# Attention in a two-layer block: the next head pair's projections cut into eight pieces and laid between the steps of the current pair

## The reference

```python
qkv = (a_lat @ w_qkv)                        # 512 x 3072: q, k, v of 16 heads of 64
kv_c = (a_ctx @ w_qkv[:, d:])                # 256 x 2048: k, v of the context
def attend_row(r):                           # 8 grid rows of 64 columns, in 4 column blocks n
    s_loc = einsum(q_row, k_slab) * scale + bias     # 8 x 32 keys around the block
    s_ctx = einsum(q_row, k_c) * scale               # 256 keys
    p = softmax(concatenate([s_loc, s_ctx], -1))
    o = einsum(p_loc, v_slab) + einsum(p_ctx, v_c)
y_lat = o @ w_o
x = x + g1 * rms_norm(y_lat, mix_post_g)     # then the feed-forward network
```

## Time and profile before

| | us |
|---|---|
| median of 3 runs | 1869.67 (1868.39 to 1873.04) |
| the profiled execution | 1864.36 |
| its span in the trace | 1862.6 |
| TensorE busy | 1703.6 (91%) |
| ACT / POOL / DVE busy | 751.0 / 796.4 / 580.4 |
| the eight pairs of the attention | 1099 to 1407 of the span |
| mean granted TensorE clock | 0.964 |

### The profile page before, as it was taken

The page is one execution under the profiler, slowest core; times in us unless marked ns, Lnnn a source line. Parts: engine busy times, 40 slices in busy tenths (PEclk is TensorE's granted clock), DMA queues, the critical chain, the costliest instruction groups (busy, mean ns, idle before and its releaser), DMA issues.

```text
span 1862.6 us, 26862 instructions
## 1 busy us (share of the span) xinstructions
PE 1703.6 (91%) x9877; PEld 1319.2 (71%) x9877; DVE 580.4 (31%) x1122; ACT 751.0 (40%) x1142; POOL 796.4 (43%) x436
## 2 busy tenths in 40 slices
PE   5799999778989999999999799999989699999996
PEld 1566555266889998888888577777767488888884
DVE  2331130154566213334300233444340533333002
ACT  2322331153667544444422233444444444444220
POOL 0444332153567974444455523333225244444551
PEclk9899999888999999999999999999999799999998
DMA  8577787621445652323233211111212033233321
GB/s 315 189 231 245 263 260 249 227 91 57 124 140 176 188 175 90 91 91 100 86 94 93 70 34 41 40 40 45 81 39 77 26 106 97 90 95 91 94 82 46
DMA packets 70655, 222.08 MB, mean 119 GB/s; under 512 B 7856, under 2 KB 15408, under 8 KB 70320
## 3 DMA queue, kind: packets, MB, share of 16 engines
q1 hardware_dynamic: 69568, 217.29, 37.2%
q10 hardware_dynamic: 1008, 3.69, 0.5%
HBM read 215.44 MB, written 5.51 MB: 119 GB/s over the span
## 4 chain that ended last, share of the span: by engine, by line
PE 75%; issue 6%; DVE 6%; DMA 5%; ACT 3%; POOL 2%; SPq 1%; DVEq 1%; ACTq 0%; POOLq 0%
PE bank L1364 21%; PE bank L1365 21%; PE bank L1366 21%; PE bank L1334 3%; PE bank L1309 2%; DMA w_raw<-in_cv_w_pw 2%; POOL w_lo L539 2%; DVE probs L1262 1%; DMA ada_raw<-in_mod_w 1%; PE bank L1492 1%; PE bank L1379 1%; PE bank L1623 1%; PE bank L1634 1%; PE bank L1611 1%; PE bank L1470 1%
## 5 line engine op out<-in xcount | busy, mean ns | idle before, releaser
L539 POOL TENSOR_TENSOR w_lo<-w_raw,w_hi 128x1024 fp32r<-128x1024 f32 (+1 forms) x284 | 671.2, 2368 | 835.3 <-ACT w_hi L683 834.8
L1364 PE MATMUL bank<-h_hi_lat,w_hi 128*128 128x512 f32 x1056 | 423.1, 401 | 8.3 <-DVE h_lo_lat L1084 8.3
L1365 PE MATMUL bank<-h_lo_lat,w_hi 128*128 128x512 f32 x1056 | 419.4, 397 | 0.0
L1366 PE MATMUL bank<-h_hi_lat,w_lo 128*128 128x512 f32 x1056 | 418.9, 397 | 0.0
L683 ACT ACTIVATE w_hi<-w_raw 128x1024 fp32r<-128x1024 f32 (+1 forms) x284 | 295.3, 1040 | 275.5 <-DMA w_raw<-in_cv_w_pw 139.8
L1364 PEld LDWEIGHTS bank<-h_hi_lat,w_hi 128*128 128x128 f32 x1056 | 199.7, 189 | 67.6 <-issue 11.3
L1366 PEld LDWEIGHTS bank<-h_hi_lat,w_lo 128*128 128x128 f32 x1056 | 199.6, 189 | 48.3
L1365 PEld LDWEIGHTS bank<-h_lo_lat,w_hi 128*128 128x128 f32 x1056 | 199.8, 189 | 46.8
L1364 PE MATMUL bank<-h_hi_ctx,w_hi 128*128 128x256 f32 x672 | 194.9, 290 | 25.3 <-DVE h_lo_ctx L1056 10.2
L1365 PE MATMUL bank<-h_lo_ctx,w_hi 128*128 128x256 f32 x672 | 190.9, 284 | 0.0
L1366 PE MATMUL bank<-h_hi_ctx,w_lo 128*128 128x256 f32 x672 | 190.8, 284 | 0.0
(11 more groups left out here) (172 smaller groups left out, 2194.2 us busy)
## 6 DMA issues: line engine op xcount, KB each, us to landing
w_raw<-in_ffn_w_up SPq DMA_DIRECT2D x132, 512.0 KB, 3.6
ada_raw<-in_mod_w SPq DMA_DIRECT2D x96, 512.0 KB, 5.5
w_raw<-in_cv_w_pw SPq DMA_DIRECT2D x48, 512.0 KB, 6.9
w_raw<-in_ffn_w_down SPq DMA_DIRECT2D x48, 448.0 KB, 3.4
w_raw<-in_ffn_w_down SPq DMA_DIRECT2D x24, 512.0 KB, 3.6
w_raw<-in_na_w_qkv SPq DMA_DIRECT2D x24, 512.0 KB, 6.1
shifted_lat<-u_lat SPq DMA_DIRECT2D x32, 270.0 KB, 4.7
shifted_ctx<-u_ctx SPq DMA_DIRECT2D x32, 142.0 KB, 2.9
```

The lines of the kernel that those rows point to most:

```text
L539: pool.tensor_tensor(wlo[s][:, 0:kt * P], raw[s][:, 0:kt * P], whi[s][:, 0:kt * P].bitcast(F32), ALU.subtract).then_inc(w_lo, 1)
L1364: pe.matmul(b, whi[s][:, w], hi[:, a], start=(first and k == 0), stop=False)
L1365: pe.matmul(b, whi[s][:, w], lo[:, a], start=False, stop=False)
L1366: ins = pe.matmul(b, wlo[s][:, w], hi[:, a], start=False, stop=(last and k == kts - 1))
```

## The change

TensorE: the products of pair m + 1 are cut into eight pieces (`pair_products`): values in two halves of four k tiles, context values, keys in two halves, context keys, queries in two halves. Piece by piece they stand between the transposes, scores and weighted sums of pair m, three to each n; the places 8 to 10 take the three parts of turn_v. Values come first, queries last (the weight blocks are loaded in that order as well). Score(n + 1) follows turn_p(2n), and score(0) of the next pair stands before the last turn_p. In the last pair the nine free places take 7 of 8 k tiles of each of the first three blocks of "o" (`o_part`), where one block was begun before. ACT: the three copies out of PSUM, each with its rounding of weights, stand behind pt_copy 1, 3 and 5; the first two exponentials of the next pair stand behind pt_copy 6 and ahead of pt_copy 7, and behind pt_copy 7. DVE: take_max goes in twos, and the first two tiles of the next pair are done before `o_lo` of this one. POOL: the bias tables come before the last `w_lo` of the pair instead of after it. Banks: scores always in 5 and 6, transposed probabilities in 7 and 3, values and queries in 0, context in 1, keys and turned values in 2.

`qkv_products` falls away whole; of it, and of other long removed runs, nothing is shown here, since the functions before stand above.

```diff
-        SCORES = [[bank[5], bank[6]], [bank[0], bank[1]]]
-        TURNED = [bank[7], bank[2]]
-        V_TURNED = bank[3]
+        V_BANK, CTX_BANK, K_BANK, Q_BANK = bank[0], bank[1], bank[2], bank[0]
+        Q_FIRST = bank[3]
+        SCORES = [bank[5], bank[6]]
+        TURNED = [bank[7], bank[3]]
+        V_TURNED = bank[2]
...
                 for j in range(ph.per):
-                    lo_ahead(ph, it, j, last)
                     mj = j // 3
                     if j % 3 == 2 and not (isinstance(it, int) and it == 0 and mj == 0):
                         for hp in range(2):
                             pool.wait_ge(s_max, it * 16 + (8 * mj - 8 + 7 + hp + 2))
                             head_bias(it * 2 + mj, hp)
+                    lo_ahead(ph, it, j, last)
             loop(pool, ph, qkv_body, cuts=(1,))
...
-            def qkv_evac(m, q, b):
-                act.wait_ge(blk, b(1))
+            def v_out(q):
+                for n in range(NB):
+                    ins = act.activation(vT[q][:, n * WIN:(n + 1) * WIN].rearrange("p (r c) -> p r c", c=KB_W),
+                                         window(V_BANK[:, 0:L], n, 0, NA_KH), ACT.Copy)
+                ins.then_inc(kv_ev, 1)
+                act.activation(vT[q][:, NB * WIN:NB * WIN + C], CTX_BANK[:, C:2 * C], ACT.Copy).then_inc(kv_ev, 1)
+            def k_out(q):
+                act.activation(kT[q][:, 0:L], K_BANK[:, 0:L], ACT.Copy).then_inc(kv_ev, 1)
+                act.activation(kT[q][:, L:L + C], CTX_BANK[:, 0:C], ACT.Copy).then_inc(kv_ev, 1)
+            def q_out(q, b=Q_BANK):
                 act.activation(qT[q][:, :].rearrange("p (n r c) -> p r n c", n=NB, c=NA_KW),
-                               bank[0][:, 0:L].rearrange("p (r n c) -> p r n c", n=NB, c=NA_KW),
+                               b[:, 0:L].rearrange("p (r n c) -> p r n c", n=NB, c=NA_KW),
                                ACT.Copy, scale=SCALE).then_inc(kv_ev, 1)
...
+            def take(out, it, mj, j, last):
+                act.wait_ge(blk, it * 6 + (ph.blk0 + 3 * mj + j + 1))
+                out(mj)
+                hi_ahead(ph, it, 3 * mj + j, last)
...
-            def attend(m, ahead):
-                exp_tile(m, 0)
-                exp_tile(m, 1)
-                ahead()
+            def attend(m, nxt=None):
                 for t in range(8):
                     pt_copy(m, t)
                     if t + 2 < 8:
                         exp_tile(m, t + 2)
+                    elif nxt:
+                        exp_tile(m + 1, t - 6)
+                    if nxt and t in (1, 3, 5):
+                        take((v_out, k_out, q_out)[t // 2], nxt[0], nxt[1], t // 2, nxt[2])
                 act.wait_ge(pv, m * 8 + 9)
...
+            def two(i, t, v_at=None):
+                take_max(i, t)
+                take_max(i, t + 1)
+                if v_at:
+                    v_at(2)
+                normalise(i, t)
+                normalise(i, t + 1)
             def attend(m, q, more=True):
...
+                i, nxt = (m,), (m + 1,)
+                two(i, 2)
+                two(i, 4)
+                take_max(i, 6)
+                take_max(i, 7)
+                normalise(i, 6)
+                if more:
+                    v_by_token(m + 1, 1 - q, 0)
+                normalise(i, 7)
+                if more:
+                    v_by_token(m + 1, 1 - q, 1)
+                    two(nxt, 0, lambda b: v_by_token(m + 1, 1 - q, b))
                 dve.wait_ge(o_hi, m + 1)
                 o = [t[:, ds(m * L, L)].rearrange("p (r n c) -> p r n c", n=NB, c=NA_KW) for t in (Olo, Ohi)]
                 b4 = bank[4][:, :].rearrange("p (n r c) -> p r n c", n=NB, c=NA_KW)
                 dve.tensor_tensor(o[0], b4, o[1].bitcast(F32), ALU.subtract).then_inc(o_lo, 1)
-                if more:
-                    v_by_token(m + 1, 1 - q, 2)
             for b in range(3):
                 v_by_token(0, 0, b)
+            two((0,), 0)
...
+            def o_begun(j, k0, k1):
...
+            def pair_products(it, mj, part):
+                s = [ph.slot(3 * mj + j) for j in range(3)]
+                lat, ctx_ = (L, Hhi[LAT], Hlo[LAT]), (C, Hhi[CTX], Hlo[CTX])
+                m = it * 2 + mj
+                def run(b, n, hi, lo, j, k0, k1):
+                    return some(b, n, s[j], hi, lo, k0, k1)
+                if part == 0:
+                    split_wait(ph, it, 3 * mj)
+                    pe.wait_ge(kv_ev, it * 10 + 5 * mj)
+                    run(V_BANK[:, 0:L], *lat, 0, 0, 4)
+                elif part == 1:
+                    run(V_BANK[:, 0:L], *lat, 0, 4, 8)
+                elif part == 2:
+                    run(CTX_BANK[:, C:2 * C], *ctx_, 0, 0, 8).then_inc(blk, 1)
+                elif part == 3:
+                    split_wait(ph, it, 3 * mj + 1)
+                    pe.wait_ge(vt_ev, it * 6 + 3 * mj)
+                    run(K_BANK[:, 0:L], *lat, 1, 0, 4)
+                elif part == 4:
+                    run(K_BANK[:, 0:L], *lat, 1, 4, 8)
+                elif part == 5:
+                    pe.wait_ge(kv_ev, it * 10 + (5 * mj + 2))
+                    run(CTX_BANK[:, 0:C], *ctx_, 1, 0, 8).then_inc(blk, 1)
+                elif part == 6:
+                    split_wait(ph, it, 3 * mj + 2)
+                    pe.wait_ge(kv_ev, it * 10 + (5 * mj + 1))
+                    run(Q_BANK[:, 0:L], *lat, 2, 0, 4)
+                elif part == 7:
+                    run(Q_BANK[:, 0:L], *lat, 2, 4, 8).then_inc(blk, 1)
+                elif part < 11:
+                    turn_v(m, mj, part - 8)
+            O_PARTS = [(0, 0, 2), (0, 2, 4), (0, 4, 7), (1, 0, 2), (1, 2, 4), (1, 4, 7), (2, 0, 2), (2, 2, 4), (2, 4, 7)]
+            def o_part(part):
+                if part >= len(O_PARTS):
+                    return
+                j, k0, k1 = O_PARTS[part]
+                if k0 == 0:
+                    split_wait(phases["o"], 0, j)
+                if part == 0:
+                    pe.wait_ge(kv_ev, 5 * KD)
+                    pe.wait_ge(vt_ev, 3 * KD)
+                    pe.wait_ge(o_lo, KD - 1)
+                elif part == 2:
+                    pe.wait_ge(o_lo, KD)
+                o_begun(j, k0, k1)
...
+            def score(m, q, n):
+                if n == 0:
+                    pe.wait_ge(kv_ev, m * 5 + 5)
                 for part in range(2):
                     for h in range(2):
                         rows_ = slice(h * HEAD_D, (h + 1) * HEAD_D)
                         keys = kT[q][rows_, L:L + C] if part else window(kT[q][rows_, 0:L], n, 0, NA_KH)
-                        if n >= 2 and part == 0:
-                            pe.wait_ge(s_max, m * 8 + (2 * n + h - 1))
-                        ins = pe.matmul(SCORES[n % 2][h][:, part * C:(part + 1) * C],
+                        if part == 0:
+                            pe.wait_ge(s_max, m * 8 + (2 * n + h + 1))
+                        ins = pe.matmul(SCORES[h][:, part * C:(part + 1) * C],
                                         qT[q][rows_, n * P:(n + 1) * P], keys, start=True, stop=True)
                         if part:
                             ins.then_inc(s_rdy, 1)
...
+            def attend(m, q, between, more=True):
                 for n in range(NB):
...
+                    between(3 * n)
+                    turn_p(m, 2 * n)
+                    if n + 1 < NB:
+                        score(m, q, n + 1)
+                    elif more:
+                        score(m + 1, 1 - q, 0)
+                    between(3 * n + 1)
+                    turn_p(m, 2 * n + 1)
+                    between(3 * n + 2)
                     weighted(m, q, n)
-                if ahead:
-                    turn_v(m + 1, 1 - q, 2)
-            qkv_products(0, 0, first=True)
+            s = [ph.slot(j) for j in range(3)]
+            products_as_made(s[0:2], chains["ffn_l"].h0, (V_BANK, K_BANK))
+            split_wait(ph, 0, 2)
+            products(Q_FIRST[:, 0:L], L, s[2], KD, Hhi[LAT], Hlo[LAT], 0, True, True).then_inc(blk, 1)
             pe.transpose(bank[7][:, 0:P], ident[:, :], ident[:, :]).then_inc(pt_tr, 1)
             pe.matmul(bank[4][0:HEAD_D, 0:2], ident[:, 0:HEAD_D], ident[:, 0:2], start=True, stop=True).then_inc(pv, 1)
+            score(0, 0, 0)
             for b in range(3):
                 turn_v(0, 0, b)
             with pe.Fori(0, ph.iters - 1) as it:
-                attend(it * 2, 0, lambda: qkv_products(it, 1))
-                attend(it * 2 + 1, 1, lambda: qkv_products(it + 1, 0))
+                attend(it * 2, 0, lambda part: pair_products(it, 1, part))
+                attend(it * 2 + 1, 1, lambda part: pair_products(it + 1, 0, part))
             last = ph.iters - 1
-            attend(2 * last, 0, lambda: qkv_products(last, 1))
-            attend(2 * last + 1, 1)
+            attend(2 * last, 0, lambda part: pair_products(last, 1, part))
+            attend(2 * last + 1, 1, o_part, more=False)
```

(25 more changed lines are left out.)

111 lines of the change are left out of this document (25 added, 86 removed).

## The result

| | before | after |
|---|---|---|
| median | 1867.97 us (6 runs) | 1850.91 us (6 runs, 1847.22 to 1853.18) |
| profiled execution, its span | 1864.36, 1862.6 | 1851.61, 1849.8 |
| a steady pair | 40.21 | 38.58 |
| end of the first products to end of "o" | 352.9 | 337.8 (1096.50 to 1434.26) |

The account below looks back on a forecast made before the run. TensorE was taken to set the time. From first products' end to the end of "o": 5.0 + 1.65 + 7 x 39.4 + 28.8 + 32.5 = 343.8 us against 352.9, 9.1 won: 1869.7 - 9.1 = 1860.6, range 1851 to 1873.

Parts of the forecast that it names:

- Part 1: TensorE's products within a pair: each cut costs 0.20 us, seven more cuts 1.4, so dense work is 37.4 us.
- part 4: Start, last pair and "o": 5.0 us to the first piece, 1.65 for lower clock, last pair 28.8, "o" 32.5.
- Rival A: Cuts of TensorE's products are free: 11.6 us more, 20.7 won, 1849; chance 0.13, including results between it and the forecast.
- Part 2: TensorE's waits on softmax in n = 0, 1, 2: pieces of 2.7 to 2.9 us cover them, all go.
- Part 3: End of a pair: TensorE waits 0.39 before W(2), 1.65 before W(3); a pair takes 39.4 us, 0.8 won.
- rival B: Pair's end longer, DVE slowed beside POOL: 4.9 us over seven pairs, 4.2 won, 1865.5; chance 0.17 with similar small slips.
- Rival C: Clock falls at each pair's end: 1.65 us a fall, eight cost 13.2, 4.1 slower, 1873.8; chance 0.08.
- Rival D: Cuts dearer at TensorE's joints through semaphore waits: 0.50 us each, 19.5 more, 10.4 slower, 1880; chance 0.12.

Follow-up runs that it names:

- the second experiment: Changed kernel with, on ACT alone, the last copy of turned probabilities put ahead of the next pair's first exponential: 1845.71 us.
- the fastest kernel: Changed kernel with piece 0 ahead of the previous pair's last weighted sum and the other pieces grouped ahead of W(0), W(1), W(2): 1832.59 us.
- the rotated one: Changed kernel with each pair's first piece of products moved ahead of the last weighted sum of the pair before: 1838.23 us.
- with three groups: Changed kernel with three pieces a pair instead of eight: all values, keys and queries ahead of weighted sums 0, 1 and 2: 1847.05 us.
- with one block of "o": Changed kernel with only the first block of "o" begun in the last pair, as in the kernel before: 1854.46 us.

## Why the forecast was too small

**Part 1, the price of a cut: this step failed.** It took one way in (0.11, behind a score) and one way out (0.09, before a weighted sum) and charged both at every cut, 0.20. By the starts the dense work of the changed pair is 38.58 - 0.39 - 1.65 = 36.54 us, not 37.4. Over the 36.0 of one block that is 0.54 for seven cuts, 0.08 each; the pairs shown of the three kernels with fewer cuts give 0.04 to 0.05 for a further one. (The 36.0 is itself added from a few rows. By it three pieces would leave 0.31 for two cuts, so either it is some 0.2 low or the pieces that end before a weighted sum are the dear ones; no run separates these.) Six of eight pieces are left before transposes, which costs nothing (0.24), and the transposes behind a product run 0.05 shorter than behind a score; that kind of joint wasn't in the rows I priced it by. The error is 0.86 a pair, 6.0 us over seven pairs, and as good as the whole gap of 6.0 between the 9.1 forecast and the 15.1 of the trace. That the two agree so closely is partly luck, as part 4 shows. Rival A (cuts free) was nearer than the forecast by the price of a cut and by the median (1849 against 1850.91); by the trace, with 20.7 won against 15.1, it was about as far off. "TensorE: Matmul & The Clock Gate" ("The mechanism") of the Trainium skill says that loads into the background weights are pulled ahead of running matmuls. Taken to mean that cuts are free, as rival A has it, it is off by 0.04 to 0.08 us a cut here, and my reading of the rows by 0.12 to 0.16.

**Part 2, covered waits: right.** None is left before turn_p, and none before a piece. Before, three groups of waits within the pairs came to 23.1 us, and 13.1 are left.

**Part 3, the end of the pair: right in mechanism and size.** Forecast 0.39 before W(2) and 1.65 before W(3). Measured behind T(5) (1210.94) and T(7) (1215.61): 0.25 and 1.50 idle, to which 0.15 each of modelled ends come. Counted from T(5)'s end, 1211.37, the tables stand at 3.1 and take_max starts at 4.07 (forecast 3.1 and 4.05); W(3) starts 5.49 after W(2) (1212.22 to 1217.71), forecast 5.45 (0.85 to 6.3). The copy behind the exponential is its releaser, as the second experiment shows. Of rival B, normalise(7) did become longer (0.87 instead of 0.49), and it takes 0.49 at the same place (1222.07) in the kernel with POOL's old order, where POOL stands idle then. That agrees with "SBUF — State Buffer" ("Who interferes with whom") of the Trainium skill, by which such a scaling and a GpSimd instruction exclude each other. But the copies of turned values on either side of it, which I had charged as well, stayed at 0.69 us, and one lengthening of 0.38 doesn't pass the score: take_max still started 1.17 after it.

**Part 4.** Start: 4.9 us to the first piece (1096.50 to 1101.44), forecast 5.0, and 1.55 for the lower clock (40.13 for the whole first pair), forecast 1.65. Last pair: 27.6 us, forecast 28.8; nine cuts at 0.20 were in it, of which 1.2 too many. "O": 33.5, forecast 32.5; here the clock fell at the first products, which no step had. In the fastest kernel, with the clock full, it is 32.5 (1381.92 to 1414.38). So the two errors of this part cancel, which is luck.

**Clock.** Rival C did not come: 1.00 in the steady pair. Its price was set too low, though: the kernel with POOL's old order pays 2.07 us a pair for it, not 1.65. The argument against it, that TensorE had stood at clock 1.00 before, passed over the last pair, whose window shows 0.86. Rival D (0.50 a cut) is out by the rows: a turn_p, which has semaphores to wait for, starts 0.24 after the last product ahead of it, where 0.235 is the usual distance.

The medians differ by 17, the traces by 15.1 in the stretch; the interval of 13 to 21 holds both.

## What to carry to other kernels

Price a cut by the joints that the new order really makes, each kind on its own (into the stream behind a score, out of it before transposes, out before a weighted sum): a sum made from the two dearest joints was 6.0 us wrong, where 9.1 had been forecast. When work is cut up to cover waits, look where the cover runs out, at the seam of two rounds; a piece of the next round moved ahead of the last wait brought another 11.3 us over the stretch (1838 against 1851 for the whole kernel). And ask for each engine off the path which of its two next jobs somebody waits for: the swapped order of two jobs on POOL carries some 40 us here.

## What the chip showed that I had not expected

- At the start of "o" TensorE stands for the same 1.54 us in all versions. In the traces of the changed kernel, the one with two cuts fewer and the rotated one the clock then falls for some 3 us (0.43 from product to product instead of 0.235); in those of the kernels with the exponentials moved, with three groups, with one block of "o", with POOL's old order, and of the fastest one it does not. From the first product of "o" to the end of the span it is 447.4 (1849.8 - 1402.4), 447.5 and 448.6 us with the fall, and 446.1 to 446.4 in the four without it that have as many products. What decides is open: the last steps ahead of "o" (two turn_p, W(3)) are the same in the changed kernel and in four of the five where it stays up. With one trace of each kernel, it isn't shown either that the kernel decides and not the execution.
- In the kernel with POOL's old order the last weighted sum of a pair, behind 5.51 us of standing, ran at the lower clock and a pair lost 2.07 us; in the changed kernel, behind 1.50 us, a pair lost nothing. At the start of "o", where 1.54 us of standing goes with either clock, the length of the standing alone doesn't tell which comes.
